# A three-layer transformer kernel: the last two row blocks by token tile, norms in halves, and norm passes moved between stages

## The chip, the cores and the metric

The kernel runs on one core of a Trainium2 chip. The metric is device time in microseconds, median of several runs; lower is better. The core has TensorE (PE, with a separate row PEld for its weight loads), VectorE (DVE), ScalarE (ACT), GpSimd (POOL) and the queue of SyncE (SP), which issues the weight loads. The engines run side by side and wait for one another by semaphores; each works through its own instructions strictly in program order.

## The reference

x is 256 tokens by 1024 channels, float32. Three parts run one after another:

- **First block.** `h = x + mixer(rms_norm(x))`, then `rms_norm` again. The mixer projects to ten streams of 1024, has a gated causal convolution and a dilated window attention over 16 heads, merges both and projects by `w_o`.
- **Layer A.** A sparse attention (12 heads: compressed, selected and window branch) beside a memory attention of 4 heads over 256 memory tokens, out projection, `layer_norm(ALPHA * x + ...)`, then a feed-forward part (2816 wide, causal convolution of three taps, gelu, gate) and a second `layer_norm`.
- **Layer B.** Block attention with shared keys and values (12 heads, here plain causal attention with a relative bias) beside memory attention, then the same two norms around a second feed-forward part.

```python
def layer_norm(x, g, b):
    xf = x.astype(jnp.float32)
    mu = xf.mean(-1, keepdims=True)
    var = jnp.square(xf - mu).mean(-1, keepdims=True)
    return ((xf - mu) * lax.rsqrt(var + LN_EPS) * g + b).astype(x.dtype)
```

## The kernel before

**Precision and weights.** All products are in the fast 32-bit format of TensorE. Each operand is split into a high part (rounded to that format) and a low part (what is left), and a product is three matmuls: high x high, high x low, low x high. The weights arrive as a stream of 300 blocks of 128 x 1024 numbers (512 KB) in a ring of three slots. For each block SyncE loads `raw`, ScalarE writes its high half `wh` (`make_high`, L402), VectorE its low half `wl` (`make_low`, L804). `refill(b)` stands for both: it puts block b + 3 into the slot of block b. ScalarE's part waits for the count `used` (block b's matmuls are done) and for the load; VectorE's part waits for ScalarE's. TensorE waits by `ready(b)` for the count of low halves, and the next load into a slot waits for the low half, too.

**Blocks.** `stationary` takes a block as eight stationary tiles and moves 256 tokens: 24 matmuls of 256 columns. `row` takes 128 rows of an output weight matrix as the moving operand: for each of two token tiles (128 tokens) and each of two halves of the columns, three matmuls of 512 columns, 12 in all, added up over many blocks in the four PSUM banks 4 to 7 (`ysum`, one pair of banks per token tile). `wide` moves weights too, for the tokens or the memory tokens. In the feed-forward parts a block's outputs are gated, split (`mh` by ScalarE, `ml` by VectorE) and multiplied by a row block; the last two row blocks stand at the end.

**Norms.** There are six: n0 at the start (of x), n1 after the first block, n2 and n3 in layer A, n4 and n5 in layer B. For n1 to n4 the steps are:

1. `norm_sum` (VectorE): when tile 0 of the last row block is done (count `half`) the sum of the residual and `ysum[0]` goes to z with its row sum (L850), when all is done tile 1 follows. In n2 to n5 a small L855 makes the mean.
2. `norm_var` (ScalarE, L416): the squares of a tile with their sum. GpSimd's `rstd` (L298, L300) turns it into the factor.
3. z is scaled (VectorE, L878; L882 in n1), one pass of 1024 columns per token tile, then VectorE's part of two refills (`fill`) follows.
4. `turn_x` (TensorE, L1421): eight transposes per token tile to PSUM. Between the two tiles stands a block of keys or values of the memory (`memory_keys`; in n3 two `wide` blocks into bank 4, for which TensorE waits until `ysum` has been read).
5. `norm_x` (VectorE) fetches column tile k = 0 to 5 from PSUM with gain and shift into `xf` (L825, L822), ScalarE those of k = 6, 7 (L435); `norm_high` (ScalarE, L427) makes the high parts `xh` from `xf`. The low parts `xl` are made by VectorE for even k (L814) and by GpSimd for odd k (`low_odd`, L312).
6. TensorE takes tile k's three products once `xl` of k is there (`x_ready`): `two_stationary` (L1365 to L1367) for the first two blocks, taking them k by k, in n1, n2 and n4; `row` in n0; products of 512 columns (L1782) in n3.

The residual itself, z times the gain plus the shift, is made off this path by `tail_step` in four passes of 1024 columns (L891, L896), for n3 in the pairs 1 to 4 of the second attention.

**Second attention.** `moba(i)`, i = 0 to 5, on TensorE: two stationary blocks (q and k of pair i), the turn of pair i - 1's probabilities (L1439), the scores of pair i (L1432), the value products of pair i - 1 (L1446). VectorE's order in a pair is: a ring low half, the copy of one head's turned probabilities, four score passes with their minimum, the low part of the output before (`o_low`), a ring low half, a norm pass (`tail_step`), and then the scaling of the probabilities (L923) that the next turn waits for. `finish` then has the eight output row blocks, with the memory attention's two pairs in between; its last two refills of VectorE stand before the norm's sum.

Of the kernel before, what the change touches and what calls it, by code (L numbers as in the profile page):

```python
# [18 lines left out]
F32 = mybir.dt.float32  # L19
# [50 lines left out]
PAIR_BANK = (5, 6, 4, 5, 6, 7, 6, 6, 6, 6)  # L70

# [37 lines left out]
def build_program(nc, a):  # L109
    ctx = ExitStack()  # L110
    with ctx:
# [3 lines left out]
        def sem(name):  # L115
# [95 lines left out]
        per_norm = {"sum": 2, "mean": 2, "var": 2, "rstd": 2, "z": 2, "x": 2, "half": 1, "off": 2,  # L211
                    "turned": KT, "xf": 6, "xf_act": 2, "xh": KT, "xl_dve": 4, "xl_pool": 4}
# [8 lines left out]
        def turned_x(nm, k):  # L221

            bk = bank[(0 if nm in ("n0", "n3") else 4) + k // 2]
            return bk[:, (k % 2) * T:(k % 2 + 1) * T]
# [29 lines left out]
        def _(sp):  # L254
# [24 lines left out]
            for t in range(NT):  # L279
                norm_wait(sp, "n5", "z", t + 1)  # L280
                sp.dma_start(a["out"][0, t * P:(t + 1) * P, :], x_tok[:, t, :]).then_inc(out_done, 16)
# [4 lines left out]
        def _(pool):  # L286
# [21 lines left out]
            def low_odd(nm):  # L308

                for k in range(1, KT, 2):  # L310
                    norm_wait(pool, nm, "xh", k + 1)
                    pool.tensor_tensor(xl[:, k, :], xf[:, k, :], xh[:, k, :].bitcast(F32), ALU.subtract  # L312
                                       ).then_inc(S[nm, "xl_pool"], 1)

# [10 lines left out]
            low_odd("n0")  # L325
# [33 lines left out]
            low_odd("n1")  # L359
# [19 lines left out]
            for nm, g, b, row in (("n2", "ln2_g_2", "ln2_b_2", 0),  # L379
# [4 lines left out]
                low_odd(nm)  # L384
# [11 lines left out]
        def _(act):  # L396
# [23 lines left out]
            def norm_high(nm, g, b):  # L420

                def high(k):
                    if k < 6:
                        norm_wait(act, nm, "xf", k + 1)
                    else:
                        norm_wait(act, nm, "xf_act", k - 5)
                    act.activation(xh[:, k, :], xf[:, k, :], ACT.Copy).then_inc(S[nm, "xh"], 1)  # L427

                for k in range(4):
                    high(k)  # L430
                norm_wait(act, nm, "turned", KT)
                for k in (6, 7):
                    if k == 7:
                        high(4)
                    act.activation(xf[:, k, :], turned_x(nm, k), ACT.Identity,  # L435
                                   scale=gbt[:, g, k:k + 1], bias=0.0 if b is None else gbt[:, b, k:k + 1]
                                   ).then_inc(S[nm, "xf_act"], 1)
                for k in range(5, KT):
                    high(k)
# [1566 lines left out]
```

## Time and profile before

| | |
|---|---|
| median of 3 runs | 991.85 us (991.31 to 992.7) |
| the profiled execution's own time | 988.38 us |
| its span in the trace | 986.7 us |
| TensorE busy | 944.5 us (96%) |
| VectorE busy | 658.9 us (67%) |
| ScalarE busy | 526.1 us (53%) |
| GpSimd busy | 83.0 us (8%) |
| mean DMA rate | 175 GB/s |

A row of the timeline begins with the start and the duration in us, then engine, line, operation, output <- input, and their shapes; equal neighbours are merged (x8); in square brackets stands how long the engine had been idle and what it waited for. Matmuls overlap: a row's duration is longer than the distance to the next start. A mean over a group is in ns. Lines are those of the kernel before.

### The profile page before, as it was taken

Reading aid. Unit: us, or ns where it says so; the run is one execution under the profiler, and the core shown is the slowest. Engines: PE = TensorE matmul, PEld = TensorE weight load, DVE = VectorE, ACT = ScalarE, POOL = GpSimd, SP = SyncE. Lnnn points to the kernel's source line nnn. Section 1 sums busy time; section 2 is a strip of 40 time slices with the busy share of each in tenths; the row PEclk is TensorE's granted clock in tenths of the full one; section 3 lists DMA queues with packets and bytes.
Section 4 is the critical chain, followed back from the end, with each engine's and each line's share of the span. In section 5 each row is a group of like instructions: output and inputs, shape, how many; then the busy total and the mean of one; then the engine's idle time right before and its main releaser. Section 6 shows DMA issues by size and latency. Waiting matters only on the chain.

```text
span 986.7 us, 19868 instructions
## 1 busy us (share of the span) xinstructions
PE 944.5 (96%) x6998; PEld 857.1 (87%) x7006; DVE 658.9 (67%) x1228; ACT 526.1 (53%) x967; POOL 83.0 (8%) x139
## 2 busy tenths in 40 slices
PE   7999999999999988989899999999999999999995
PEld 5899999999999877757799999988887689999995
DVE  5566666666666766975776666666677677666665
ACT  5445555555444557764655555555665465555552
POOL 3000000000000102640100000002000010000001
PEclk9999999999999999999999999999999999999998
DMA  7555555556555465314467555555555346655551
GB/s 250 183 182 181 181 183 179 176 183 216 185 183 184 146 215 165 120 53 139 157 191 227 184 188 190 191 190 156 186 162 192 107 133 197 224 191 191 188 185 74
DMA packets 48227, 172.90 MB, mean 175 GB/s; under 512 B 6031, under 2 KB 6479, under 8 KB 48060
## 3 DMA queue, kind: packets, MB, share of 16 engines
q1 hardware_dynamic: 44732, 159.78, 49.2%
q0 software_dynamic: 3456, 12.61, 4.3%
q8 instruction: 24, 0.39, 0.2%
q14 instruction: 15, 0.12, 0.0%
HBM read 171.29 MB, written 1.07 MB: 175 GB/s over the span
## 4 chain that ended last, share of the span: by engine, by line
PE 81%; DVE 7%; ACT 6%; DMA 3%; issue 2%; POOL 1%; SPq 0%; POOLq 0%; DVEq 0%; ACTq 0%
PE bank L1353 17%; PE bank L1354 17%; PE bank L1355 17%; PE ysum L1401 7%; PE ysum L1403 7%; PE ysum L1402 7%; DMA sb_raw<-in_stream 2%; ACT sb_wh L402 2%; DVE sb_wl L804 2%; PE bank L1432 2%; PE ysum L1439 1%; ACT sb_pr L447 1%; PE ysum L1446 1%; DVE sb_sc L915 1%; DVE sb_z L850 1%
## 5 line engine op out<-in xcount | busy, mean ns | idle before, releaser
L804 DVE TENSOR_TENSOR sb_wl<-sb_raw,sb_wh 128x1024 fp32r<-128x1024 f32 x300 | 366.5, 1223 | 166.0 <-ACT sb_wh L402 165.0
L1353 PE MATMUL bank<-sb_xh,sb_wh 128*128 128x256 f32 x1360 | 383.6, 282 | 0.9 <-DVE sb_t_a L1261 0.9
L1354 PE MATMUL bank<-sb_xl,sb_wh 128*128 128x256 f32 x1360 | 380.3, 280 | 0.0
L1355 PE MATMUL bank<-sb_xh,sb_wl 128*128 128x256 f32 x1360 | 380.3, 280 | 0.0
L402 ACT ACTIVATE sb_wh<-sb_raw 128x1024 fp32r<-128x1024 f32 x300 | 314.5, 1053 | 108.6 <-PE ysum L1403 49.3
L1353 PEld LDWEIGHTS bank<-sb_xh,sb_wh 128*128 128x128 f32 x1360 | 256.4, 189 | 9.6 <-issue 3.7
L1355 PEld LDWEIGHTS bank<-sb_xh,sb_wl 128*128 128x128 f32 x1360 | 258.2, 190 | 0.0
L1354 PEld LDWEIGHTS bank<-sb_xl,sb_wh 128*128 128x128 f32 x1360 | 255.3, 188 | 1.6
L1401 PE MATMUL ysum<-sb_wh,sb_mh 128*128 128x512 f32 x208 | 81.1, 390 | 0.9 <-DVE sb_ml L814 0.9
L1403 PE MATMUL ysum<-sb_wh,sb_ml 128*128 128x512 f32 x208 | 80.9, 389 | 0.0
L1402 PE MATMUL ysum<-sb_wl,sb_mh 128*128 128x512 f32 x208 | 80.9, 389 | 0.0
L712 ACT ACTIVATE sb_mh<-sb_t_c 128x256 fp32r<-128x256 f32 x44 | 18.3, 416 | 90.2 <-DVE sb_t_c L1269 90.2
L702 ACT ACTIVATE sb_t_a<-bank,sb_convf 128x256 f32<-128x256 f32 x44 | 24.9, 566 | 48.8 <-PE bank L1355 46.5
L447 ACT ACTIVATE sb_pr<-sb_sc,sb_mx 128x128 f32<-128x128 f32 x80 | 35.4, 444 | 23.7 <-DVE sb_mx L915 23.7
L1403 PEld LDWEIGHTS ysum<-sb_wh,sb_ml 128*128 128x128 f32 x208 | 39.0, 188 | 8.1
L1401 PEld LDWEIGHTS ysum<-sb_wh,sb_mh 128*128 128x128 f32 x208 | 39.0, 188 | 7.5 <-issue 1.2
L1402 PEld LDWEIGHTS ysum<-sb_wl,sb_mh 128*128 128x128 f32 x208 | 39.0, 188 | 6.2
L298 POOL TENSOR_SCALAR sb_st<-sb_st 128x1 f32<-128x1 f32 x12 | 4.2, 351 | 419.6 <-ACT sb_pr L416 415.2
L1353 PE MATMUL bank<-sb_mixh,sb_wh 128*128 128x256 f32 x128 | 36.2, 282 | 0.0
L1354 PE MATMUL bank<-sb_mixl,sb_wh 128*128 128x256 f32 x128 | 36.0, 281 | 0.0
L1355 PE MATMUL bank<-sb_mixh,sb_wl 128*128 128x256 f32 x128 | 36.0, 281 | 0.0
L814 DVE TENSOR_TENSOR sb_ml<-sb_t_c,sb_mh 128x256 fp32r<-128x256 f32 x44 | 18.7, 425 | 24.2 <-ACT sb_mh L712 24.2
(265 smaller groups left out, 1388.6 us busy)
## 6 DMA issues: line engine op xcount, KB each, us to landing
sb_raw<-in_stream SPq DMA_DIRECT2D x300, 512.0 KB, 3.3
sb_bias<-rel_rows POOLq DMA_DIRECT2D x12, 384.0 KB, 3.8
sb_bias<-in_alibi POOLq DMA_DIRECT2D x8, 256.0 KB, 3.1
sb_gb<-in_ln_g POOLq DMA_DIRECT2D x4, 512.0 KB, 4.9
sb_gb<-in_ln_b POOLq DMA_DIRECT2D x4, 512.0 KB, 6.4
sb_x_tok<-in_x SPq DMA_DIRECT2D x2, 512.0 KB, 4.0
sb_memf<-in_mem_t POOLq DMA_DIRECT2D x1, 1024.0 KB, 6.5
out<-sb_x_tok SPq DMA_DIRECT2D x2, 512.0 KB, 2.6
```

The source lines that it names most:

```text
L402: act.activation(wh[slot][:, :, :], raw[slot][:, :, :], ACT.Copy).then_inc(split_h, 1)
L447: act.activation(to[:, branch, h, cols], src, ACT.Exp, bias=mx[:, c:c + 1], scale=-1.0, accum_out=den[:, c:c + 1]).then_inc(S[ph, "exp"], 1)
L702: act.activation(t_a[:, :], bank[0][:, 0:T], ACT.Identity, bias=convf[:, layer, bass.ds(i, 1), 3], scale=convf[:, layer, bass.ds(i, 1), 2] ...
L804: dve.tensor_tensor(wl[slot][:, :, :], raw[slot][:, :, :], wh[slot][:, :, :].bitcast(F32), ALU.subtract).then_inc(split_l, 1)
L814: dve.tensor_tensor(dst, src, high, ALU.subtract).then_inc(s, 1)
L1353: pe.matmul(out, wh[slot][:, k, :], mov_h(k), start=k == 0, stop=False)
L1354: pe.matmul(out, wh[slot][:, k, :], mov_l(k), start=False, stop=False)
L1355: last = pe.matmul(out, wl[slot][:, k, :], mov_h(k), start=False, stop=k == KT - 1)
L1401: pe.matmul(out, th[:, t * P:(t + 1) * P], hw, start=start, stop=False)
L1402: pe.matmul(out, th[:, t * P:(t + 1) * P], lw, start=False, stop=False)
L1403: last = pe.matmul(out, tl[:, t * P:(t + 1) * P], hw, start=False, stop=stop)
L1432: last = pe.matmul(outs[h][:, cols], q[r, t * P:(t + 1) * P], k[r, 0:lead + (t + 1) * P], start=True, stop=True)
```

## The change

- **Token tile order** (`last_rows`): the last two row blocks before n1 to n5 go tile 0 of both, then tile 1 of both, instead of block by block. `half` is counted after tile 0 of both. Before the second block's tile 0 TensorE waits for that block's own operand. VectorE's refill of the first of them moves from ahead of the sums to behind them (`soon`); ScalarE's stays ahead of the squares.
- **z in halves**: each tile's scaling is two passes of 512 columns, and the transposes wait for each half.
- **High parts from PSUM**: ScalarE makes all eight `xh` directly from PSUM with gain and shift, then `xf` of k = 6, 7. VectorE fetches `xf` of k = 0 to 5 (in n1, n2 and n4 in the order 4, 5, 0 to 3) and makes all eight low parts; GpSimd's `low_odd` is gone.
- **x products in two passes** (`two_stationary`, `x_rows`): first those of `xh`, for all k of the block or blocks, which wait for `xh` alone, then those of `xl`.
- **Cover**: the second block of memory keys is cut in two, one half between the two tiles' transposes and one behind; in n3 the first memory value block comes ahead of the transposes, into bank 3, and the second is cut by token tile.
- **n4**: ScalarE's one refill goes ahead of its high parts.
- **Norm passes**: n3's four `tail_step` passes leave the attention pairs for `finish`, between its refills, and in each pair the scaling of the probabilities moves ahead of `o_low` and the ring's low half.

```diff
+                for k in range(KT):
+                    norm_wait(act, nm, "turned", k // 2 * 2 + 2)
+                    if k in (4, 5) and nm not in ("n0", "n3"):
+                        norm_wait(act, nm, "xf", 2)
+                    act.activation(xh[:, k, :], turned_x(nm, k), ACT.Identity, scale=gbt[:, g, k:k + 1],
+                                   bias=shift[k]).then_inc(S[nm, "xh"], 1)
...
+                if nm in ("n0", "n3"):
+                    for k in FETCHED[nm]:
+                        fetch(k)
+                        low_of(k)
+                        if k == 0 and between is not None:
+                            between()
+                else:
+                    for k in FETCHED[nm][:4]:
+                        fetch(k)
+                    low_of(0)
+                    for k in FETCHED[nm][4:]:
+                        fetch(k)
+                    for k in range(1, 6):
+                        low_of(k)
+                for k in (6, 7):
+                    low_of(k)
...
+                if soon is not None:
+                    refill(0, soon)
...
+                    for n in range(2):
+                        part = z[:, t, n * 512:(n + 1) * 512]
+                        if centred:
+                            dve.tensor_scalar(part, part, st[:, 4 + t:5 + t], st[:, 10 + t:11 + t],
+                                              ALU.add, ALU.mult).then_inc(S[nm, "z"], 1)
...
                 for h in range(2):
                     dve.wait_ge(S["p5", "s"], i * 2 + (h + 1))
                     score_min("p5", 0, h, bank[3 + h], NO_KEY)
+                dve.wait_ge(S["p5", "exp"], i * 4 + 4)
+                chain.link(dve.tensor_scalar(deng[:, 0:4], den[:, 0:4], TINY, None, ALU.max))
+                chain.link(dve.reciprocal(rden[:, 0:4], deng[:, 0:4]))
+                for h in range(2):
+                    scale_probs("p5", 0, h, rden)
                 if i:
                     o_low("p5", i - 1, i - 1, 7)
                 refill(0, b + 1)
-                if 0 < i < 5:
-                    tail_step("n3", i - 1)
...
+                for k in range(KT):
+                    norm_wait(pe, nm, "xh", k + 1)
+                    for n in range(2):
+                        out, s = bank[n][:, 0:T], slot_of(b + n)
+                        pe.matmul(out, wh[s][:, k, :], xh[:, k, :], start=k == 0, stop=False)
+                        pe.matmul(out, wl[s][:, k, :], xh[:, k, :], start=False, stop=False)
...
+            def last_rows(b, first, second, half, second_made=()):
+
+                ready(b + 1)
+                row_tile(slot_of(b), *first, 0, False, False)
+                ready(b + 2)
+                for made in second_made:
+                    pe.wait_ge(*made)
+                row_tile(slot_of(b + 1), *second, 0, False, True).then_inc(half, 1)
+                row_tile(slot_of(b), *first, 1, False, False).then_inc(used, 1)
+                row_tile(slot_of(b + 1), *second, 1, False, True).then_inc(used, 1)
...
+                keys(0)
+                turn_x(nm, 0)
+                keys(1, 0, KT // 2)
+                turn_x(nm, 1)
+                keys(1, KT // 2, KT)
```

## Rows read from the trace of the kernel before

**Rows 1.** The page: the span, and the shares of the chain that ended last.
```profile
span 986.7 us, 19868 instructions
...
PE 81%; DVE 7%; ACT 6%; DMA 3%; issue 2%; POOL 1%; SPq 0%; POOLq 0%; DVEq 0%; ACTq 0%
```

**Rows 2.** The page's groups of instructions: busy us, mean ns of one, idle before.
```profile
L804 DVE TENSOR_TENSOR sb_wl<-sb_raw,sb_wh 128x1024 fp32r<-128x1024 f32 x300 | 366.5, 1223 | 166.0 <-ACT sb_wh L402 165.0
...
L402 ACT ACTIVATE sb_wh<-sb_raw 128x1024 fp32r<-128x1024 f32 x300 | 314.5, 1053 | 108.6 <-PE ysum L1403 49.3
...
L814 DVE TENSOR_TENSOR sb_ml<-sb_t_c,sb_mh 128x256 fp32r<-128x256 f32 x44 | 18.7, 425 | 24.2 <-ACT sb_mh L712 24.2
```

**Rows 3.** Groups by form: x's high parts from PSUM (ScalarE), fetches (VectorE).
```profile
L435 ACT ACTIVATE sb_pt<-ysum,sb_gbt 128x256 f32<-128x256 f32 x6 | 3.1, 519 | 0.0
...
L825 DVE TENSOR_SCALAR sb_pt<-ysum,sb_gbt 128x256 f32<-128x256 f32 x12 | 6.0, 537 | 1.1 <-PE ysum L1421 1.1
```

**Rows 4.** Timeline of PE at norm n2: start us, duration us, instruction.
```profile
463.27 0.50 PE L1401 MATMUL ysum<-sb_wh,sb_mixh 128*128 128x512 f32 x1
...
468.66 0.39 PE L1403 MATMUL ysum<-sb_wh,sb_mixl 128*128 128x512 f32 x1
...
468.88 0.28 PE L1353 MATMUL bank<-sb_memh,sb_wh 128*128 128x256 f32 x1
...
471.59 0.28 PE L1355 MATMUL bank<-sb_memh,sb_wl 128*128 128x256 f32 x1
...
473.10 1.09 PE L1421 MATMUL ysum<-sb_ident,sb_z 128*128 128x128 f32 x8 [1.22 <-DVE sb_z L878]
...
478.79 0.36 PE L1365 MATMUL bank<-sb_xh,sb_wh 128*128 128x256 f32 x1 [0.98 <-DVE sb_xl L814]
...
486.20 0.39 PE L1353 MATMUL bank<-sb_xh,sb_wh 128*128 128x256 f32 x1 [0.47 <-DVE sb_t_a L1261]
```

**Rows 5.** Timeline of VectorE and ScalarE in the same stretch.
```profile
464.58 0.42 DVE L814 TENSOR_TENSOR sb_mixl<-bank,sb_mixh 128x256 fp32r<-128x256 f32 x1
...
468.57 1.21 DVE L850 SCALAR_TENSOR_TENSOR sb_z<-sb_x_tok,ysum 128x1024 f32<-128x1024 f32 x1
...
470.02 1.15 ACT L416 ACTIVATE sb_pr<-sb_z,sb_st 128x1024 f32<-128x1024 f32 x1 [2.62 <-DVE sb_st L855]
...
472.23 0.81 DVE L878 TENSOR_SCALAR sb_z<-sb_z,sb_st 128x1024 f32<-128x1024 f32 x1 [0.92 <-POOL sb_st L300]
```

**Rows 6.** Timeline: the starts that end the other norms' stretches.
```profile
17.43 2.42 DVE L804 TENSOR_TENSOR sb_wl<-sb_raw,sb_wh 128x1024 fp32r<-128x1024 f32 x2 [0.49 <-ACT sb_wh L402]
...
19.19 0.39 PE L1401 MATMUL ysum<-sb_wh,sb_xh 128*128 128x512 f32 x1
...
346.65 0.38 PE L1381 MATMUL bank<-sb_wh,sb_xh 128*128 128x256 f32 x1 [1.05 <-DVE sb_wl L804]
...
681.72 0.50 PE L1782 MATMUL ysum<-sb_wh,sb_xh 128*128 128x512 f32 x1 [0.50 <-DVE sb_wl L804]
...
796.72 0.38 PE L1353 MATMUL bank<-sb_xh,sb_wh 128*128 128x256 f32 x1 [0.47 <-DVE sb_t_a L1261]
```

**Rows 7.** Timeline of the second attention's pairs.
```profile
700.00 0.38 PE L1353 MATMUL bank<-sb_xh,sb_wh 128*128 128x256 f32 x1
...
712.88 1.22 DVE L891 TENSOR_TENSOR sb_x_tok<-sb_z,sb_gb 128x1024 f32<-128x1024 f32 x1
...
715.03 1.01 PE L1439 MATMUL ysum<-sb_ident,sb_pr 128*128 128x128 f32 x6 [0.46 <-DVE sb_pr L923]
...
717.14 0.66 PE L1446 MATMUL ysum<-sb_pt,sb_memf 128*64 128x256 f32 x4 [0.24 <-issue]
...
745.48 0.38 PE L1353 MATMUL bank<-sb_xh,sb_wh 128*128 128x256 f32 x1
```

**Rows 8.** Timeline of GpSimd in the last norm.
```profile
977.69 1.23 POOL L298 TENSOR_SCALAR sb_st<-sb_st 128x1 f32<-128x1 f32 x1 [140.84 <-ACT sb_pr L416]
```

**Rows 9.** Windows: us, busy time of PE, PEld, DVE, ACT, POOL, granted clock, DMA.
```profile
12.00:15.50 3.50, 3.48 (x8) 2.76 (x9) 3.32 (x7) 1.92 (x6) 2.33 (x2) 0.51 0.73 238
```

More of the change, by code:

```diff
@@ L1349, in _, with stationary @@
         def _(pe):
-            def stationary(slot, out, mov_h, mov_l):
-                for k in range(KT):
+            def stationary(slot, out, mov_h, mov_l, k0=0, k1=KT):
+                for k in range(k0, k1):
                     pe.matmul(out, wh[slot][:, k, :], mov_h(k), start=k == 0, stop=False)
@@ L1388, in wait @@
                 def wait(k):
[L1389 to L1406 removed]
+                    norm_wait(pe, nm, "xh", k + 1)
@@ new lines, in wait, with row_tile @@
+                    norm_wait(pe, nm, "xl", k + 1)
+                return wait
+            def row_tile(slot, th, tl, t, start, stop, bank7_read=None):
+                for n in range(2):
+                    out = bank[4 + 2 * t + n][:, :]
+                    if bank7_read is not None and t == n == 1:
+                        pe.wait_ge(*bank7_read)
+                    hw = wh[slot][:, 4 * n:4 * n + 4, :].rearrange("p k c -> p (k c)")
+                    lw = wl[slot][:, 4 * n:4 * n + 4, :].rearrange("p k c -> p (k c)")
+                    pe.matmul(out, th[:, t * P:(t + 1) * P], hw, start=start, stop=False)
+                    pe.matmul(out, th[:, t * P:(t + 1) * P], lw, start=False, stop=False)
+                    last = pe.matmul(out, tl[:, t * P:(t + 1) * P], hw, start=False, stop=stop)
+                return last
@@ new lines, in row @@
+            def row(slot, th, tl, start, stop, bank7_read=None):
+                for t in range(NT):
+                    last = row_tile(slot, th, tl, t, start, stop, bank7_read)
+                last.then_inc(used, 1)
+            def last_rows(b, first, second, half, second_made=()):
[7 more added lines that the diff above has]
+                row_tile(slot_of(b + 1), *second, 1, False, True).then_inc(used, 1)
@@ L1465, in _ @@
                 ready(k + 1)
-                x_ready("n0")(k)
-                row(slot_of(k), xh[:, k, :], xl[:, k, :], k == 0, k == KT - 1)
+                x_rows("n0", slot_of(k), [(k, 0, t, n) for t in range(NT) for n in range(2)],
+                       lambda t, n: bank[4 + 2 * t + n], n_first=True)
             pe.wait_ge(consts_in, 16 * 7)
@@ L1729, in finish @@
                 memory_out(ph, 1)
-                rows(6)
-                pe.wait_ge(S[ph, "ol"], 2)
-                rows(7)
+                last_rows(r0 + 6, (oh[:, 6, :], ol[:, 6, :]), (oh[:, 7, :], ol[:, 7, :]), half, ((S[ph, "ol"], 2),))
             pe.wait_ge(S["p3", "fill"], 3)
```

199 lines of the change are left out of this document (87 added, 112 removed).

## Prediction, made before the change was run

> **What bounds the kernel now.** The page first: TensorE is on 81% of the chain that ended last [rows 1], so time is won only where TensorE waits. The groups of instructions give the prices of the two other engines' routine work: each 512 KB weight block costs ScalarE 1.05 us (its high half) and VectorE 1.22 us (its low half) [rows 2], against 2.7 to 2.8 us of TensorE (24 products of 256 columns from 468.88 to 471.59 are 0.118 us each, 12 of 512 columns 0.23 each [rows 4]). VectorE is idle a third of the time, but it works in program order, so what matters is what stands ahead of the operation TensorE needs. Then the timeline, for TensorE's starts that carry an idle time. They stand in three kinds of place: around each norm, in the pairs of the second attention, and in stages that the change doesn't touch.
>
> **A norm, worked through (n2).** Today the two last row blocks run 463.27 to 468.88; the first sum (DVE L850) starts at 468.57, the squares (L416) at 470.02, z (L878) at 472.23, the transposes at 473.10 after 1.22 us idle, the next block's products at 478.79 after 0.98 us idle, and the feed-forward stage proper at 486.20 [rows 4, 5]. What the change does to this, step by step:
>
> 1. *Token tile order.* The first block's tile 0 takes six products, to 464.68. The second block's tile 0 needs the last low halves of the attention output, finished at 464.58 + 0.42 = 465.00 [rows 5]; before, TensorE came to them only at 466.0. So a new wait of 0.37 us appears, and the four pieces end at 465.05 + 18 x 0.228 = 469.16 instead of 468.88: a loss of 0.28. The first sum can start a lag of 0.26 after 466.42: 466.68, against 468.57.
> 2. *What stands between.* The first block's slot is now free only at 467.79, and ScalarE still makes that slot's new high half before the squares: 467.99 to 469.05. The squares start at 469.05 (0.97 earlier, not 1.9). z could follow after today's 2.21 us (470.02 to 472.23 [rows 5]), at 471.26. VectorE isn't free: second sum 469.42 to 470.82 with its mean, then the low half that the change puts behind the sums, 1.15 more: 471.97. So z comes 0.26 earlier.
> 3. *z in halves.* Tile 0's pass of 1024 columns is 0.81 [rows 5]. A 256-column VectorE pass is 0.54 [rows 3], with PSUM as source, so a half of 512 lies between 0.41 (half the pass) and 0.68 (midway between the two rows); I take 0.55. Transposes start at 471.97 + 0.58 = 472.55, against 473.10, and the other half is there when the first four are done. VectorE pays 0.15 to 0.3 more per tile, in time it has.
> 4. *Key products as cover.* Behind the first transposes TensorE now has half a block, the second transposes, half a block: 0.84 + 1.41 + 0.84 + 1.41 = 4.5, to 477.05. That cover is what hides ScalarE and VectorE here; without it the first high half would be waited for about 0.8 us.
> 5. *High half from PSUM.* Today's path is fetch, high, low before the first product. Now ScalarE reads PSUM directly, 0.52 per 256 columns (L435), pitch about 0.45: x's high halves come from 475.3 to 479. TensorE needs them only from 477.05, in steps of 0.47 (four products each), so it doesn't wait. The high products, 32 of them, end at 480.83.
> 6. *Low halves, VectorE alone.* Two ring lows end at 476.5; the fetches (0.54) and lows (0.43 [rows 2, 3]), dependent ones at 0.92 per k and then 0.34 each, end at 481.9. The last is wanted at 482.45. No wait, end 482.7; today's end is 478.79 + 48 x 0.118 = 484.5 plus. The conv chain and 486.20 move with it: 484.2. **n2: -2.0 us.** GpSimd's four subtractions, which go, were not what TensorE waited for most.
>
> **The other norms, in the same way, to the row after which TensorE is bound again [rows 6].**
> - n1 (no mean): the new wait is 0.73, since the last gated product is finished only 2.1 us into the rows; transposes 330.66 instead of 330.73; but the products after it start at 335.2 instead of 336.44, and the ring's next low half follows at 341.0. The chain over the compressed blocks to 346.65 moves to 345.1: **-1.5**. The stage after it is a chain of load, high, low, load, so it moves as a whole.
> - n3: new wait 0.23; with the memory values in a bank of its own TensorE starts at once (1.0 us idle goes), transposes -0.6, first x product 673.5. The block after these four waits for VectorE: six fetch-and-low steps of 0.92, two lows, then its ring low ends 680.45. TensorE idles 1.5 us, and 681.72 becomes 680.5: **-1.25**.
> - n4: rows -0.4 on the new wait, no ring work ahead of z but one low, x products at 787.1, 796.72 becomes 794.7: **-2.0**.
> - n0: ScalarE's high half of x comes 1.1 us sooner. But VectorE now has eight lows instead of four ahead of the third weight block's low half, which starts at 17.43 today [rows 6]: 13.35 (end of the second block's) + 5 steps of 0.85 + two of 0.34 = 18.28. TensorE's third block starts at 19.54 instead of 19.19: **+0.35**. Before that it idles some 1.4 us.
> - n5: the first sum comes 1.1 us sooner, the second 0.2 later. The tail is set by GpSimd's small operations, which take 1.23 instead of 0.2 beside VectorE's passes [rows 8]; the first now falls beside the sum that reads PSUM, the second doesn't move: **-0.3** (0 to -0.6).
>
> **The second attention's pairs.** Six blocks of pair work start at 700.00 and, the last, 745.48: five periods of 9.10 us [rows 7]. In one, 48 products take 5.56, the turn 0.74 undisturbed, the scores 0.76, the value products 0.81: 7.87. The rest is waiting: the turn at 715.03 idles 0.46 and then runs 1.01 for its two heads, because the probabilities are scaled only after a low half and the norm pass of 1.22 at 712.88; the value products at 717.14 wait for a copy that queues behind another low half [rows 7]. With the scaling first, probabilities are ready 5.9 us after the turn of the pair before, less than 7.87; VectorE's own work is 5.9 per period, ScalarE's 5.6, so TensorE is the bound. Gain 5 x 1.23 = 6.1; I take **-6.0**. From below: the idle times that the profile itself shows at these ten places add to 3.0, which is the other end. The four passes of 1.22 move into the output rows after it, between VectorE's low halves, where it idles 1.2 to 1.8 each time; if that cover were gone, each pass would cost up to 1.2.
>
> **Sum.** +0.35 - 1.5 - 2.0 - 1.25 - 6.0 - 2.0 - 0.3 = -12.7. The profiled execution took 988.38, so 975.7; the median of the runs is 3.47 above it, which I carry along: **979.2 us** (-1.3%).
>
> **Two rules weighed.** The clock was at 0.51 of full from 12.0 to 15.5, right after TensorE had idled 2 us at the first norm [rows 9]: the 1.2 GHz level, and such a stretch costs half its length, 1.75. My sum leaves this fall where it is and the 1.75 of a second one goes into the range. The Trainium skill (TensorE: Matmul & The Clock Gate, Part 1) has it that the clock is throttled by default and that idleness brings this back; by that rule the changed first norm, with a new idle stretch before its third block, could fall a second time, while every other norm idles less than now. The other: z's pass is 0.81 for 1024 columns [rows 5]. The Trainium skill (VectorE: DVE Perf Modes, The TRN2 errata) charges a fixed part per instruction and gives an estimate of (58 + 256)/0.96 = 0.33 us for a half of 512 columns; by that each norm would start its transposes 0.2 us sooner. By the same formula the whole pass would be 0.59, below the row, so the row is kept.
>
> **Rivals.**
> - *As worked out*, 0.57: 979.2, own range 976.5 to 981.5.
> - *The clock falls a second time at the first norm*, 0.06: the new idle stretch of 1.4 us, before the third block, is followed by 3.5 us at half the clock, as the one of 2 us was [rows 9]: 980.9. Against it: idle stretches of 1.22 and 0.98 at n2 left the products there at 0.118 [rows 4]. This is where the page on TensorE's clock, cited above, would take it.
> - *The norms give back what they gain*, 0.2: VectorE, which takes over all low halves of x, two half passes and the ring's delayed low, is late by another 1 us at each norm. For it: my n0 and n3 already end in waits for it. Against: at n1, n2 and n4 it has 0.5 to 1 us in hand. The norms give -1.5 instead of -6.7: 984.4.
> - *The attention gives only its visible idle time*, 0.11: a wait for k's copy or for the next probabilities takes its place: -3.0 instead of -6.0, 982.2.
> - *Slower*, 0.03: the low half put behind the sums delays z and, through the ring, the load for that slot at all five norms. It decides when it costs 12.7/5 = 2.5 us more at each than worked out; with 3 us it gives 994. Against it: the pass is 1.22 and the ring holds two other blocks.
> - Within 0.2% (under 2 us, about what these runs can tell from nothing): 0.02. Mixed small results hold the last 0.01.
>
> Faster 0.95, same 0.02, slower 0.03. The range 976.5 to 985 takes in both partial cases and the 1.75.
>
> **What would show it.** Attention periods of 7.9 us, no idle time at the turns. Output rows with a new wait of 0.2 to 0.7 ahead of the second block's tile 0. Transposes only 0.1 to 0.7 sooner at each norm but the next products 1.2 to 2 sooner and without a wait. A wait for VectorE's low half ahead of the third block at the start and of the third value block at n3. It would be wrong if ScalarE's reads of PSUM were slower than 0.55, if VectorE's half passes were near 0.7, or if the clock fell at other norms.

## The result, and the profile after

The changed kernel takes 978.95 us (median of 4 runs, 978.58 to 979.72), the kernel before beside it 991.68: a ratio of 0.9877, 95% interval [0.9851, 0.9904]. The forecast was 979.2, "faster". A second set of runs gave 977.38 against 989.18, 0.9894 [0.9874, 0.9913]. The median agrees with the forecast to 0.25 us; the terms agree less well, and part of the agreement is luck. That is what the rest is about.

The profiled execution took 979.72 us, its span is 978.1 (before: 986.7). The page of after, to be held against [rows 1, 2]:

```profile
span 978.1 us, 19996 instructions
...
PE 84%; DVE 6%; DMA 4%; ACT 2%; issue 2%; POOL 0%; SPq 0%; POOLq 0%; ACTq 0%; DVEq 0%
...
L790 DVE TENSOR_TENSOR sb_wl<-sb_raw,sb_wh 128x1024 fp32r<-128x1024 f32 x300 | 365.6, 1223 | 152.7 <-ACT sb_wh L396 151.5
...
L396 ACT ACTIVATE sb_wh<-sb_raw 128x1024 fp32r<-128x1024 f32 x300 | 314.8, 1054 | 126.3 <-PE ysum L1436 51.4
```

The price of a weight block is what it was; TensorE's share of the chain rose from 81 to 84%, and GpSimd's fell from 1% to nothing. (Lines moved: the ring's low half is now L790, TensorE's rows L1434 to L1436, transposes L1470.)

**Norm n2**, TensorE, after [rows 4]:

```profile
464.37 0.50 PE L1434 MATMUL ysum<-sb_wh,sb_mixh 128*128 128x512 f32 x1
...
466.25 0.47 PE L1434 MATMUL ysum<-sb_wh,sb_mixh 128*128 128x512 f32 x1 [0.23 <-DVE sb_mixl L800]
...
470.46 0.28 PE L1363 MATMUL bank<-sb_memh,sb_wh 128*128 128x256 f32 x1
...
473.73 1.11 PE L1470 MATMUL ysum<-sb_ident,sb_z 128*128 128x128 f32 x8 [0.28 <-DVE sb_z L884]
...
478.31 0.28 PE L1376 MATMUL bank<-sb_xh,sb_wh 128*128 128x256 f32 x1
...
481.93 1.98 PE L1381 MATMUL bank<-sb_xl,sb_wh 128*128 128x256 f32 x16
...
485.49 0.38 PE L1363 MATMUL bank<-sb_xh,sb_wh 128*128 128x256 f32 x1 [0.70 <-DVE sb_t_a L1273]
```

Counted from the first of the last two rows' products (463.27 before, 464.37 after): the rows take 6.09 us instead of 5.61, since the second block's tile 0 waits; the transposes start at 9.36 instead of 9.83; the products of x at 13.94, with no idle time, instead of 15.52; the last x products end at 19.4 (481.93 + 16 x 0.113 = 483.7), and the feed-forward stage starts at 21.12 instead of 22.93. VectorE, ScalarE and the second of GpSimd's two operations that make the factor of tile 0, in the same stretch [rows 5]:

```profile
471.84 0.57 POOL L304 TENSOR_TENSOR sb_st<-sb_st,sb_half 128x1 f32<-128x1 f32 x1
472.00 1.22 DVE L790 TENSOR_TENSOR sb_wl<-sb_raw,sb_wh 128x1024 fp32r<-128x1024 f32 x1
473.13 1.00 DVE L884 TENSOR_SCALAR sb_z<-sb_z,sb_st 128x512 f32<-128x512 f32 x2
...
476.48 1.93 ACT L421 ACTIVATE sb_xh<-ysum,sb_gbt 128x256 fp32r<-128x256 f32 x4 [1.22 <-PE ysum L1470]
```

z starts without idle time right behind the ring's low half, 0.7 us after the factor is ready (471.84 + 0.57 = 472.41): it is VectorE's queue, not the sum of squares, that sets it. Four high halves from PSUM take 1.93 us.

**The start**, VectorE, TensorE and the clock [rows 6, 9]. First the timeline of after, then its windows (columns as in [rows 9]):

```profile
17.93 3.49 DVE L790 TENSOR_TENSOR sb_wl<-sb_raw,sb_wh 128x1024 fp32r<-128x1024 f32 x3
...
19.21 0.50 PE L1411 MATMUL ysum<-sb_wh,sb_xh 128*128 128x512 f32 x1 [2.72 <-DVE sb_wl L790]
```

```profile
12.00:15.50 3.50, 3.50 (x17) 2.88 (x16) 3.40 (x7) 2.93 (x8) 0.00 (x0) 1.00 0.92 320
16.50:19.20 2.70, 0.00 (x0) 0.00 (x0) 2.67 (x6) 1.91 (x2) 0.00 (x0) 1.00 0.07 29
20.00:24.00 4.00, 4.00 (x12) 3.12 (x11) 1.42 (x2) 0.14 (x1) 0.00 (x0) 0.58 0.73 260
399.00:403.00 4.00, 4.00 (x25) 3.24 (x22) 3.54 (x26) 2.17 (x9) 3.94 (x7) 0.59 0.38 135
```

TensorE does nothing from 16.5 to 19.2 while VectorE is busy 2.67 of 2.70 us; behind this, from 20 to 24, the granted clock is 0.58, and again in the first part of the sparse attention, at 399.

**The second attention**, first score product of pairs 2 to 6, after [rows 7]: the distances are 7.97, 7.98, 7.98 and 7.97, where before they are 9.13, 9.11, 9.12 and 9.31.

```profile
705.27 0.37 PE L1481 MATMUL bank<-sb_k_s,sb_q_s 64*128 64x128 f32 x1
...
712.49 0.82 PE L1488 MATMUL ysum<-sb_ident,sb_pr 128*128 128x128 f32 x6
713.24 0.37 PE L1481 MATMUL bank<-sb_k_s,sb_q_s 64*128 64x128 f32 x1
...
737.17 0.37 PE L1481 MATMUL bank<-sb_k_s,sb_q_s 64*128 64x128 f32 x1
```

The turn starts without an idle time.

**A table by stage.** Each column is one profiled execution; a stage is the distance between two starts of TensorE in its timeline: (a) the first product of the first block's pairs (36.72 before), (b) the end of the pairs (259.15), (c) the chain behind n1 (346.65), (e) the last value products of the sparse attention (438.89), (f) the feed-forward stage (486.20), (g) the third value block at n3 (681.72), (i) the second feed-forward stage (796.72), then the span's end. "again" is a second profile of the same, unedited kernel. An asterisk marks a stage in which the windows show a stretch at a granted clock of about 0.5. (Every execution has one more, up to its end, but TensorE's last product is over by then.)

| | before | again | after | again |
|---|---|---|---|---|
| to a (n0) | 36.72* | 36.23 | 38.45* | 38.90* |
| a to b | 222.43 | 222.11 | 222.11 | 221.90 |
| b to c (n1) | 87.50 | 87.40 | 85.99 | 86.17 |
| c to e | 92.24 | 92.70 | 93.45* | 91.46 |
| e to f (n2) | 47.31 | 47.47 | 45.49 | 45.48 |
| f to g (n3) | 195.52 | 195.51 | 194.96 | 194.41 |
| g to i (pairs, n4) | 115.00* | 114.58 | 107.84 | 107.61 |
| i to end (n5) | 189.98 | 190.00 | 189.81 | 189.77 |
| span | 986.7 | 986.0 | 978.1 | 975.7 |

### The profile page after: what moved, and what is told of

Its sections match the earlier page's. It is cut to its first block, busy times and chain, and to the rows that moved or that the text cites. A ratio compares the mean times of both kernels' runs of the same rounds, so it can differ in the third digit from the quotient of the medians.

```text
span 978.1 us, 19996 instructions
## 1 busy us (share of the span) xinstructions
PE 943.0 (96%) x6998; PEld 855.9 (88%) x7006; DVE 664.0 (68%) x1258; ACT 528.0 (54%) x967; POOL 65.9 (7%) x119
## 4 chain that ended last, share of the span: by engine, by line
PE 84%; DVE 6%; DMA 4%; ACT 2%; issue 2%; POOL 0%; SPq 0%; POOLq 0%; ACTq 0%; DVEq 0%
PE bank L1363 18%; PE bank L1364 17%; PE bank L1365 17%; PE ysum L1434 6%; PE ysum L1436 6%; PE ysum L1435 6%; DMA sb_raw<-in_stream 4%; DVE sb_wl L790 2%; PE bank L1481 2%; PE ysum L1488 2%; ACT sb_wh L396 1%; PE ysum L1495 1%; PE ysum L1411 1%; PE ysum L1412 1%; PE ysum L1415 1%
## 5 line engine op out<-in xcount | busy, mean ns | idle before, releaser
L790 DVE TENSOR_TENSOR sb_wl<-sb_raw,sb_wh 128x1024 fp32r<-128x1024 f32 x300 | 365.6, 1223 | 152.7 <-ACT sb_wh L396 151.5
L1434 PE MATMUL ysum<-sb_wh,sb_mh 128*128 128x512 f32 x208 | 81.4, 391 | 1.9 <-DVE sb_ml L800 1.2
L1436 PE MATMUL ysum<-sb_wh,sb_ml 128*128 128x512 f32 x208 | 80.9, 389 | 0.0
L1434 PEld LDWEIGHTS ysum<-sb_wh,sb_mh 128*128 128x128 f32 x208 | 39.0, 188 | 9.5 <-issue 3.4
L1436 PEld LDWEIGHTS ysum<-sb_wh,sb_ml 128*128 128x128 f32 x208 | 39.0, 188 | 8.2
L1270 DVE SCALAR_TENSOR_TENSOR sb_t_a<-bank,sb_convf,sb_t_a 128x255 f32<-128x255 f32 x44 | 21.2, 481 | 18.3 <-ACT sb_t_a L688 18.2
```

What stands on the lines that cost most here:

```text
L790: dve.tensor_tensor(wl[slot][:, :, :], raw[slot][:, :, :], wh[slot][:, :, :].bitcast(F32), ALU.subtract).then_inc(split_l, 1)
L1270: cf.link(dve.scalar_tensor_tensor(out=t_a[:, 1:T], in0=bank[0][:, 0:T - 1], scalar=convf[:, layer, bass.ds(i, 1), 1], in1=t_a[:, 1:T], op ...
L1434: pe.matmul(out, th[:, t * P:(t + 1) * P], hw, start=start, stop=False)
L1436: last = pe.matmul(out, tl[:, t * P:(t + 1) * P], hw, start=False, stop=stop)
```

## The experiments

All comparisons are with the kernel before, run between them on the same chip. Three chips were used; the median of before was 988.55, 989.18 and 990.17 on them, its runs between 986.8 and 993.3 (one run of 5285 us left out).

### The two halves of the change

`pairs_alone` is the kernel before with the attention's part only; `norms_alone` the changed kernel with the pairs as before:

```diff
 # pairs_alone, on the kernel before
+                dve.wait_ge(S["p5", "exp"], i * 4 + 4)
+                ... scale_probs("p5", 0, h, rden)
                 if i:
                     o_low("p5", i - 1, i - 1, 7)
                 refill(0, b + 1)
-                if 0 < i < 5:
-                    tail_step("n3", i - 1)
 # and tail_step("n3", 0 to 3) between the refills of finish
```

> The kernel before with only the second attention's part of the change (scaling of the probabilities ahead of the output's low part and the ring's low half; the four norm passes in the output rows behind). Theory: TensorE becomes the bound of a pair, period 7.9 us instead of 9.1, 6.0 us faster than before (about 985.7 beside 991.7); the value products lose their wait too. Rival (only the idle time that the profile of before shows goes, since k's copy or the copy of the turned probabilities takes the place): 3.0 us faster, period 8.5.

> The changed kernel with the second attention as before. Theory (both parts add up): the six norms give 6.7 us against before, so about 985.0 and 6 us slower than the changed kernel. Rival (the profiles of the two kernels differ by 8.7 and not by 12.7 us, so the norms are worth only 2.5): about 989.

Measured: the pairs alone 982.27 us, 0.9937 [0.9924, 0.9951]; the norms alone 984.15, 0.9951 [0.9933, 0.9969]. Of the table's stages the pairs alone move g to i, to 109.08 (114.58 in the profile of before without a low clock: -5.5), and the others by at most 0.7 us either way; the distance of the score products is 7.98. The norms alone give 86.16, 45.47, 194.40 and 113.16 for n1, n2, n3 and n4 (-1.2, -2.0, -1.1 and -1.4) and 38.44 at the start (+2.2), with the clock low from 20 to 24 as in after. Both theories were met: both halves are real and they add up.

### What makes the pairs shorter

`pairs_scale` moves only the scaling ahead and leaves the norm passes in the pairs; `pairs_tail` moves only the norm passes out:

```diff
 # pairs_scale
+                ... scale_probs("p5", 0, h, rden)
                 if i:
                     o_low("p5", i - 1, i - 1, 7)
                 refill(0, b + 1)
                 if 0 < i < 5:
                     tail_step("n3", i - 1)
-                ... scale_probs("p5", 0, h, rden)
```

> The kernel before with one half of the pairs' change: the scaling of the probabilities ahead of the output's low part and the ring's low half; n3's four norm passes stay in pairs 1 to 4, behind that low half. Theory (the wait for VectorE at the turn is a matter of what stands ahead of the scaling, so that each half of the change removes most of it): VectorE's round is then 6.0 of work, 1.4 of waiting for the exponentials and 1.2 for the norm pass, 8.4 to 8.6 against the 9.10 of before and 7.98 with both halves: 3 to 4 us faster than before, against about 6 with both. Rival A (the order alone does it, since the pass is hidden under TensorE's products): 5.5 to 6 faster. Rival B (the ring's low half, now later by the scaling and the norm pass, is what TensorE waits for next): within 1.5 us of before.

> The kernel before with the other half: the four norm passes stand between the refills of the output rows, the scaling stays behind the ring's low half. Theory: the scaling comes 1.2 us sooner at pairs 1 to 4, the turn no longer waits and takes 0.74 instead of 1.01: 4 to 5.5 us faster than before, nearly all of the 6. Rival (both halves are needed, since the output's low part and the ring's low half still stand ahead): 2 to 3 us faster, periods of 8.5.

Measured: 985.21 us, 0.9958 [0.994, 0.9975], and 984.86, 0.9953 [0.9933, 0.9972]. g to i is 110.75 and 110.81: each half gives 3.8 us of the 5.5 (4.2 and 4.7 by the ratios, 5.0 and 5.3 between the medians). The distances between the score products are 7.16, 8.17, 8.56, 7.97, 8.75 with the scaling ahead, and 7.69, 8.32, 7.98, 8.30, 7.98 with the passes gone. Where each falls short the timelines show, first of `pairs_scale`, then of `pairs_tail`:

```profile
713.94 1.22 DVE L891 TENSOR_TENSOR sb_x_tok<-sb_z,sb_gb 128x1024 f32<-128x1024 f32 x1
715.08 1.22 DVE L804 TENSOR_TENSOR sb_wl<-sb_raw,sb_wh 128x1024 fp32r<-128x1024 f32 x1
...
716.22 0.55 DVE L1315 COPY sb_pt<-ysum 128x384 f32<-128x384 f32 x1
...
716.87 0.66 PE L1446 MATMUL ysum<-sb_pt,sb_memf 128*64 128x256 f32 x4 [0.32 <-issue]
```

```profile
720.14 1.23 DVE L804 TENSOR_TENSOR sb_wl<-sb_raw,sb_wh 128x1024 fp32r<-128x1024 f32 x1 [0.53 <-ACT sb_wh L402]
...
721.69 1.01 DVE L923 TENSOR_SCALAR sb_pr<-sb_pr,sb_rden 128x128 f32<-128x128 f32 x4
722.62 1.22 DVE L804 TENSOR_TENSOR sb_wl<-sb_raw,sb_wh 128x1024 fp32r<-128x1024 f32 x1
...
723.75 0.55 DVE L1322 COPY sb_pt<-ysum 128x384 f32<-128x384 f32 x1
...
724.40 0.66 PE L1451 MATMUL ysum<-sb_pt,sb_memf 128*64 128x256 f32 x4 [0.24 <-issue]
```

With the scaling ahead, a norm pass and the next low half stand back to back, so that low half ends late, and the copy of the turned probabilities behind it too (716.22 + 0.55 = 716.77): the value products wait 0.32 us, in another pair 0.51. With the passes gone, the scaling stands behind a low half that itself idles 0.53 us for ScalarE, the next low half follows it, and again the copy is late: the value products wait 0.24 to 0.29 us in every second pair. From the second turn on the turn itself waits in neither kernel. The theory's 3 to 4 for the first was met in the stage; its 4 to 5.5 for the second was met by the runs and missed by 0.2 in the stage. Each half alone takes away most of the wait, so the two gains overlap and don't add.

### The order of the last rows

`block_order` is the changed kernel with the last two row blocks block by block again:

```diff
-                row_tile(slot_of(b), *first, 0, False, False)
+                row(slot_of(b), *first, False, False)
...
-                row_tile(slot_of(b), *first, 1, False, False).then_inc(used, 1)
```

> The changed kernel with the last two row blocks in the old order again, block by block; VectorE's refill stays behind the sums. Theory: the token tile order only turns into a wait, because ScalarE's high half stands ahead of the squares and VectorE's low half ahead of z: without it the rows lose their new waits of 0.83, 0.40, 0.32, 0.38 and 0.3 us at n1 to n5, the sum of tile 0 starts some 0.9 us later and z about 0.3 us earlier: 1 to 2 us faster than the changed kernel. Rival (the earlier first sum carries through to the transposes): 0.9 to 1.1 us per norm slower, 4 to 5 us in all.

Measured: 979.13 us, 0.9906 [0.9891, 0.9921], against 0.9877 and 0.9894 of the changed kernel: not to be told apart, and neither expectation was right. By stages it gives 86.01, 45.86, 194.75 and 107.83 where the changed kernel (`after_again`) has 86.17, 45.48, 194.41 and 107.61, and 190.04 against 189.77: the differences are -0.2, 0.4, 0.3, 0.2 and 0.3, 1.0 us in all, little above what a stage without a low clock differs between two profiles of one kernel (up to 0.6). The order by itself earns little because what it wins for the first sum, the ring's high half takes back ahead of the squares: counted from the first of the last two rows' products, the squares at n2 start at 5.88 with it and at 5.96 without. And even this 1.0 isn't the order's alone, because `block_order` has a cost of GpSimd's that the changed kernel is spared; first it, then `norms_alone`, where the same stretch is undisturbed:

```profile
467.85 1.22 DVE L790 TENSOR_TENSOR sb_wl<-sb_raw,sb_wh 128x1024 fp32r<-128x1024 f32 x1
...
467.99 1.14 POOL L302 TENSOR_SCALAR sb_st<-sb_st 128x1 f32<-128x1 f32 x1 [2.99 <-ACT sb_pr L410]
```

```profile
469.26 0.18 POOL L302 TENSOR_SCALAR sb_st<-sb_st 128x1 f32<-128x1 f32 x1 [2.90 <-ACT sb_pr L410]
```

An operation on one column took 1.14 us instead of 0.18 and ended when VectorE's pass over two SBUF operands ended (467.99 + 1.14 = 469.13; 467.85 + 1.22 = 469.07). z then waited 0.74 us for the factor. The same happens at n1, n3 and n4 (1.26, 1.14 and 1.14). What the order would be worth without it was not separated.

### The products in two passes, and z in halves

`one_pass` takes the first x blocks' products k by k again at n1, n2 and n4, each waiting for its low half, and at n0 and n3 the products of one column tile wait for both its halves, too; `z_whole` scales z in one pass of 1024 columns:

```diff
 # one_pass, in two_stationary and x_rows
-                    norm_wait(pe, nm, "xh", k + 1)
+                    x_ready(nm)(k)
...
-                for k in range(KT):
-                    x_ready(nm)(k)
-                    for n in range(2): ... the products of xl
```

> The changed kernel with the products of the first x blocks in one pass, each k waiting for its low half as before, at n1, n2 and n4; all else unchanged. Theory (the high halves from PSUM bring time only because the products of xh alone run while VectorE still makes xl): at n1, n2 and n4 each, the first x product waits 2 to 3 us more and the stage's end comes 1.3 to 1.5 later, the norm's gain is gone there: 4 to 5 us slower, 983 to 984. Rival (the gain of the norms comes from the order of the transposes and the half passes of z, and the last low half sets the end either way): under 1 us slower.

> The changed kernel with z scaled in one pass of 1024 columns per token tile again. Theory (0.81 for the whole against a first half of 0.55, and a second half that is there in time): the first transposes of each norm start 0.25 us later, of which nearly all is left at the stage's end: 1 us slower than the changed kernel over the norms. Rival (behind z the memory keys' products and the ring cover such a shift): within 0.3 us in every stage.

`one_pass`: 984.74 us, 0.995 [0.9932, 0.9969], 7.4 us above the unedited kernel run beside it (977.38). Its stages at n1 and n2 are 87.30 and 47.89, +1.1 and +2.4, and g to i is 110.99, +3.4, with a stretch at low clock in it. Not all of the 7.4 is the edit's: the profile has two more such stretches from c to e, where the stage is 3.7 longer behind the products that the edit changes, and over the runs the mean granted clock goes from 0.987 to 0.996. The three runs at 0.993 and more took 981.99 to 982.87, about 5 us above the unedited kernel, as the theory had it. TensorE's starts at n2 and n4:

```profile
481.39 0.36 PE L1376 MATMUL bank<-sb_xh,sb_wh 128*128 128x256 f32 x1 [1.66 <-DVE sb_xl L800]
...
482.64 0.36 PE L1376 MATMUL bank<-sb_xh,sb_wh 128*128 128x256 f32 x1 [0.30 <-DVE sb_xl L800]
...
786.10 0.55 PE L1376 MATMUL bank<-sb_xh,sb_wh 128*128 128x256 f32 x1 [2.20 <-ACT sb_xh L421]
```

Without the separate pass nearly all of n1's gain is lost and more than n2's: with VectorE making all eight low halves, k by k waiting is worse than it was before the change (47.31). The theory had the mechanism; its 1.3 to 1.5 per norm was short at n2. `z_whole`: 979.23, 0.99 [0.9882, 0.9917]; by stages +0.1, +0.5, +0.1, +0.4 and +0.2 at n1 to n5, 1.4 in all against the theory's 1, but unevenly spread: at n1 and n3 it is covered, as the rival had it. Medians can't tell it from the changed kernel.

### The start

`start_order` takes the low halves of weight blocks 2 and 3 between those of x, after k = 2 and 4, not behind all eight. `odd_lows_gpsimd` gives the low halves of odd k back to GpSimd, at all norms.

```diff
 # start_order
-            norm_x("n0", 0, None, lambda: make_low(1, 2))
-            make_low(2, 3)
-            for k in range(KT - 1):
+            norm_x("n0", 0, None, {0: lambda: make_low(1, 2), 2: lambda: make_low(2, 3),
+                                   4: lambda: refill(0, 0)})
+            for k in range(1, KT - 1):
```

> The changed kernel with VectorE's low halves of weight blocks 2 and 3 taken between the low parts of x at the first norm (after k = 2 and k = 4) instead of behind all eight. Theory: the idle stretch of 2.7 us ahead of the third block goes, and with it the low clock behind it: 2.9 + 1.7 = 4.6 us faster than the changed kernel's profile, all blocks at 2.73 us from 10.7 us on. Rival (the loads of blocks 3 to 5 then become the bound): 1 to 2 us faster.

> The changed kernel with the low halves of x for odd k made by GpSimd again at all norms. Theory (VectorE alone is the late one where the products are taken k by k, n0 and n3, and nowhere else): VectorE has four lows of 0.34 to 0.43 less at n0 and at n3, so the third weight block's low half is 1.5 us sooner at n0 (the 2.90 us between two starts of TensorE there falls under 1.5) and the value block at n3 up to 1.4 sooner; n1, n2 and n4 within 0.2 of the changed kernel: 2 to 3 us faster, 976 to 977. Rival (GpSimd's passes of two inputs shut VectorE out and are slower, each 0.6 or more, so that both engines lose what VectorE saves): x's products wait at n1, n2 and n4 as well, 2 to 4 us slower, 981 to 983.

`start_order`: 974.19 us (973.73 to 976.18), 0.9861 [0.9844, 0.9879], the fastest of all, though its interval still overlaps that of the changed kernel; the trace is what shows the gain. The stage to (a) is 34.34 us, 4.1 and 4.6 less than in the two profiles of the changed kernel (theory 4.6) and 2.6 to 2.9 less than in two profiles with the changed order and no low clock; TensorE has no gap over 0.6 us from its first product to (a). Two windows of it:

```profile
12.00:16.00 4.00, 4.00 (x19) 3.30 (x18) 3.85 (x7) 3.37 (x9) 0.00 (x0) 1.00 0.95 297
20.00:24.00 4.00, 4.00 (x19) 3.28 (x18) 3.26 (x5) 1.21 (x2) 0.00 (x0) 1.00 0.57 184
```

`odd_lows_gpsimd`: 980.04, 0.9906 [0.9888, 0.9924]. The third block starts 2.22 us after the start of the row before it instead of 2.90 (the theory had under 1.5), and n3 gains 0.8 us; but n1, n2 and the stage of n4 lose 0.8, 0.6 and 1.4. TensorE at n4:

```profile
783.84 0.47 PE L1397 MATMUL bank<-sb_xl,sb_wh 128*128 128x256 f32 x2 [0.95 <-POOL sb_xl L320]
```

Theory and rival each had half of it. GpSimd's subtractions took 0.74 to 0.85 us where VectorE left room and up to 1.3 each elsewhere (three in 3.89), against VectorE's 0.42.

### Both kernels once more, and a last combination

`before_again` and `after_again` are unedited. `best_b` is `start_order` with ScalarE's squares of tile 0 ahead of the ring's high half, and VectorE's ring low half between z of tile 0 and z of tile 1.

> The kernel before once more, unedited, for a second profile. Theory (where the clock falls differs from execution to execution, at the first norm above all): stages without a fall repeat to 0.2 us (87.50 at n1, 47.31 around n2, 97.57 for the pairs), while the start (36.72) and the stages that held a fall differ by up to 1.75 us. Rival (the falls belong to places of the program): the clock is low again from 12.0 to 15.5 and nowhere else at the start.

> The changed kernel once more, unedited, for a second profile of it on the same chip as the runs beside it. Theory (the clock falls at varying places after TensorE idles 1.4 us or more): the time is within 2 us of 979, the profile's stages without such a fall repeat to 0.2 us (85.99 from open banks to the chain at n1, 45.49 around n2, 90.39 for the pairs), and the 1.7 us at the first norm and the 1.5 us in the first attention pair of the first profile need not come back. Rival (both are fixed losses of the change): both stages are as long as in the first profile, first block's pairs starting at 38.45, first attention 59.49.

> The changed kernel with two edits. At n0 the low halves of weight blocks 2 and 3 are taken between x's low halves, after k = 2 and k = 4 (4 to 5 us faster alone than the changed kernel's 978.95). At n1 to n4 ScalarE's squares of tile 0 come ahead of its high half for the ring, and VectorE's low half for the ring between z of tile 0 and z of tile 1. Theory (in the changed kernel ring work of 1.05 and 1.15 us stands ahead of z at each norm): z of tile 0 comes 0.4 to 1 us sooner at each, of which 0.3 to 0.5 is left at the stage's end, since the ring's block is then later: 972.5 (971 to 973.5). Rival (the ring's block is what sets the end of the stage behind the norm): no faster than the 974.2 of the first edit alone, 974 to 976.

`before_again` took 987.79 us and has no stretch at low clock at all before TensorE's last product. `after_again` repeats every stage of after within 0.6 us but c to e, which has no low clock now and is 2.0 shorter; it does have the one from 20 to 24. Windows, first of `before_again`, then of `after_again`:

```profile
12.00:16.00 4.00, 4.00 (x18) 3.29 (x19) 3.30 (x7) 2.57 (x8) 2.46 (x3) 1.00 0.68 253
20.00:24.00 4.00, 4.00 (x20) 3.26 (x19) 0.84 (x1) 0.35 (x1) 0.00 (x0) 1.00 0.92 332
...
787.00:791.00 4.00, 3.02 (x26) 2.81 (x25) 3.90 (x9) 2.83 (x7) 1.48 (x2) 1.00 0.00 0
```

```profile
20.00:24.00 4.00, 4.00 (x12) 3.19 (x11) 1.88 (x2) 0.00 (x0) 0.00 (x0) 0.59 0.71 219
399.00:403.00 4.00, 4.00 (x39) 3.67 (x36) 3.64 (x30) 3.08 (x13) 4.00 (x8) 1.00 0.38 135
```

`best_b` took 975.33 (973.7 to 982.28), 0.9869 [0.9842, 0.9896]: no faster than `start_order`, the rival's side. Its stages at n1 to n4 are 86.04, 45.74, 194.82 and 108.33, -0.1, +0.3, +0.4 and +0.7 against the changed kernel. z of tile 0 does start earlier (at n2 5.8 us behind the second block's first product instead of 6.9), and TensorE's transposes 0.5, but the stage's end doesn't follow. At n4 the ring's low half, at 776.26, again shut out the small operation of tile 1's factor:

```profile
776.26 1.22 DVE L790 TENSOR_TENSOR sb_wl<-sb_raw,sb_wh 128x1024 fp32r<-128x1024 f32 x1
...
776.78 0.76 POOL L302 TENSOR_SCALAR sb_st<-sb_st 128x1 f32<-128x1 f32 x1 [1.84 <-ACT sb_pr L412]
...
778.80 1.12 PE L1470 MATMUL ysum<-sb_ident,sb_z 128*128 128x128 f32 x8 [1.36 <-DVE sb_z L882]
```

## Why the prediction was right, and where it was off

Measured terms are differences of stages between profiles without a stretch at low clock, `before_again` and `after_again` where nothing else is said.

| term | predicted | measured |
|---|---|---|
| n0 | +0.35 | +0.7 to +1.0 without, +2.2 to +2.7 with the low clock |
| n1 | -1.5 | -1.2 |
| c to e, behind n1 | 0 | -1.2 (see below) |
| n2 | -2.0 | -2.0 |
| n3 | -1.25 | -1.1 |
| pairs | -6.0 | -5.5 (`pairs_alone`) |
| n4 | -2.0 | -1.4 to -1.5 |
| n5 | -0.3 | -0.2 |

- **Pairs.** The mechanism and nearly the size: the distance is 7.98, not 7.87. The prediction took TensorE's bare work; 0.1 us more is left between the steps. Of the two ends, 3.0 of visible idle time and 6.1 worked out from the work itself, the second was the nearer: a late start also lengthens what overlaps it (a turn of 1.01 instead of 0.82). The rival that only the visible idle time comes back fell with 109.08 in place of 111.6.
- **n2, step by step.** New wait: 0.40 between two products, 0.37 predicted. Transposes 0.47 sooner, 0.55 predicted. z half: two in 1.00, 0.54 for one in the mean, so 0.50 to 0.55 as taken; the Trainium skill's formula (VectorE: DVE Perf Modes, The TRN2 errata) gives 0.33, as an estimate, and the row decides against it. High halves at a distance of 0.47, 0.45 predicted, and no wait for them. The last x product was where the forecast had it (19.4 us behind the rows' first product). The stage's end came 0.2 later: the gate's chain behind the last x product, with 0.70 of idle time instead of 0.47, was moved "with it" and had been part-hidden before.
- **n1, n3, n4.** New waits of TensorE at the second block's tile 0: 0.83, 0.32 and 0.38 between products (0.73, 0.23, 0.4 predicted). At n3 TensorE waits 1.1 us for the value block's low half (1.5 predicted). n4's -2.0 was sized against a row of before that has a stretch at low clock in it: at 787 to 791 in that one execution, and not in the second, where g to i is 0.4 shorter. Taken against that, n4 is 0.5 less.
- **n0, the step that failed.** "Before that it idles some 1.4 us": it idled 2.72. I had left the early low clock of [rows 9] where it was, so the two blocks ahead of the third would take their time. In after and `after_again` the clock was at full from 12, TensorE was done sooner and waited for the same low half; the third block's start, 19.21, is even earlier than the 19.54 of the forecast. What follows is the rival "the clock falls a second time", changed: it falls once, but later, where nothing hides it. In before a fall at 12 cost 0.5 to 0.6 us (36.72 against 36.23, 36.13 and 36.08 in three executions without), as TensorE would have waited anyway; at 20 to 24 TensorE is bound, and the start is 38.4 to 38.9 against 37.0 and 37.2 in the two executions with this order and no fall (`one_pass`, whose edit touches n0's products, too, and `block_order`). The Trainium skill (TensorE: Matmul & The Clock Gate, Part 1) says that idleness brings the throttle back; of six executions with this order three agree, with 2.7 us of idle ahead of the fall in after; `block_order` idles the same 2.72 us there and shows none, `one_pass` 1.38 and none. In the sixth, `z_whole`, the clock was low from 12 to 16: there TensorE waited 1.09 us and began the third block at 19.76, about what the prediction had (1.4 and 19.54).
- **The sum.** Predicted for the profile was 975.7, measured 979.72 and, again, 977.38. By the first and third column of the table the 4.0 that are missing lie at the start (1.4), from c to e (1.2, the low clock there), from g to i (0.8), at n3 (0.7, of which the second profile shows 0.1) and at n2 and n5 (0.3), less 0.3 from a to b. That the median was hit all the same is in part luck: before's runs lay 3.5 us above its profile, and I carried this along; after's lie 0.8 below its own. The runs say where most of such a difference comes from: among the 14 runs of before beside `pairs_scale` the four with a mean granted clock of 0.997 took 987.5 to 988.3 us, the five at 0.990 to 0.993 took 990.3 to 993.3. So the scatter goes with the granted clock (one stretch that lacks 1.7 us takes 0.0017 off the mean), and no term of the sum counts how often it falls. It isn't the whole: `pairs_alone`'s five runs lie within 0.6 us at clocks of 0.992 to 0.996, and that isn't settled.
- **c to e.** 92.2 to 93.0 in four executions with the norms as before, without a fall, and 91.2 to 91.5 in five of the six with the changed norms (92.4 in `start_order`). The chain of loads behind n1 doesn't just move as a whole, as I had it. The shift is there before TensorE's longest wait of the stage (1.3 to 1.8 us, for a copy of turned probabilities): that row comes 50.5 to 51.3 us behind (c) in the four, 49.4 to 49.6 in the five, and 50.6 in `start_order`. Between (c) and this row TensorE waits three or four times, 0.4 us or more each, for low halves of the ring, at other places in each execution; which of these waits becomes shorter was not traced.

No slower case came near. The low half put behind the sums does hold z back, at n1 to n4 in after by 0.6 to 0.7 us behind the factor, but nothing like the 2.5 us per norm at which that rival decides; and `best_b`, which takes z of tile 0 first, gains nothing.

## What to carry to other kernels

When a producer is late, look what the queue of its engine holds ahead of it: four passes of 1.2 us that "fit" into idle time cost more than their own idle time where they stood ahead of a scaling. Splitting a product into the part that can start at once and the part that waits can be what a norm's gain hangs on: without it nearly all of the gain at n1 was gone and more than all at n2. Before sizing a gain against one profiled execution, take a second one of the same kernel: a stretch at low clock in one stage can be 0.4 or 2.0 us of it.

## What the runs showed of the hardware

- The granted clock falls to about 0.5 for 3 to 4 us at a time (12 to 16, 20 to 24, 399 to 403, 785 to 791), and added up over windows of 1 us each such stretch lacks 1.7 us of full clock. The same kernel shows it in one execution and not in the other: before two and none, after two and one. What it costs depends on the place: 0.2 to 0.6 us where TensorE would have waited anyway, 1.2 to 2.2 at the start and in the sparse attention of after, where it was bound. In after it followed idle stretches of 2.7 and 1.5 us; other executions have the same stretches and no fall. Behind TensorE's last product the clock was low in all 14 profiles.
- GpSimd's factor operation on a single column (L298, L302) takes 0.18 to 0.19 us alone, and the same when it starts during VectorE's sum of an SBUF and a PSUM operand (39 times in 14 profiles). Started during VectorE's low half for the ring, two SBUF operands, it takes 0.71 to 1.26 (8 times), and in the last norm 1.10 and 1.23 [rows 8]; it ends 0.04 to 0.06 us after that pass. Started during the scaling of z, one SBUF operand, it takes 0.2 to 0.6, and in most cases it ends with that pass, too.
